# Retention's values in one token-major tile, a flag of their own for the rotation's banks, and a root table loaded earlier

## The reference, cut to what matters

```python
h = rmsnorm(x, mix_norm[l])
u = h @ w_in[l]                        # 1024 -> 3488 columns
(c_x, c_b, c_c, rw_r, rw_k, rw_v, rw_wd_f, rw_wd_b, rw_ad_f, rw_ad_b, rw_gd,
 rt_q, rt_k, rt_v, rt_g, ml_qa, ml_kva) = jnp.split(u, split_points, axis=-1)
...
y_ret = retention_mixer(rt_q, rt_k, rt_v, rt_g, positions, ret_gn_g[l])
y_mla = mla_mixer(ml_qa, ml_kva, positions, mla_q_a_norm[l], mla_q_b[l], mla_kv_a_norm[l], mla_kv_b[l])
```

## The kernel before

| ahead of p | TensorE | VectorE | ScalarE |
|---|---|---|---|
| 6 | MLA's projections (800, 802, 805) | copies of them (978 to 980) | a copy (932) |
| 7 | rotations of MLA (813) and of retention (821) into banks 3 to 7 | MLA's rope (986 to 995) | |
| 8 | | retention's rope (1001, 1002, 1004) | silu of the gates (935) |
| 9 | MLA's scores (829) into banks 3 to 6 | row maxima (1008, 1010) | exponentials (941) |
| 10 | retention's scores (840) | decay (1016), softmax division (1027) | |
| 11 | retention's output (850) | convolution | a square (946) |
| 12 | sums (858), transposes of probabilities (868) | retention's end (1056 to 762) | square root (949), copies (953) |

## Time and profile before

### The profile page before, as it was taken

How to read it: one execution, slowest core, us unless ns; L and a number is a source line. 1 busy time by engine, 2 the same in 40 slices (tenths; PEclk the granted TensorE clock), 3 DMA queues, 4 the chain that set the end, 5 groups by cost and what they waited for, 6 DMA issues and landing times.

```text
span 2914.4 us, 49969 instructions
## 1 busy us (share of the span) xinstructions
PE 2703.1 (93%) x20144; PEld 2382.9 (82%) x20144; DVE 1911.3 (66%) x1750; ACT 1419.3 (49%) x1330; POOL 84.6 (3%) x82
## 2 busy tenths in 40 slices
PE   8999989999999989986999896899999989999997
PEld 8988888989998879976999795687777777777876
DVE  4555765555555854555556645688878878888886
ACT  4343513343343513342336532566757666666665
POOL 6000005000000000000000000000000000000000
PEclk9999999999999999997999998899999999999999
DMA  7553213545553205542555400799989989999995
GB/s 274 181 191 130 93 46 130 187 159 174 187 189 107 94 17 184 187 156 87 187 187 146 145 3 8 283 338 344 344 292 340 342 296 336 337 342 336 341 346 197
DMA packets 340994, 602.08 MB, mean 207 GB/s; under 512 B 11968, under 2 KB 178752, under 8 KB 340672
## 3 DMA queue, kind: packets, MB, share of 16 engines
q1 hardware_dynamic: 333184, 590.84, 59.2%
q10 hardware_dynamic: 7616, 8.58, 0.9%
HBM read 598.34 MB, written 1.05 MB: 206 GB/s over the span
## 4 chain that ended last, share of the span: by engine, by line
DMA 54%; PE 22%; DVE 12%; ACT 8%; DVEq 2%; issue 1%; SPq 1%; another core or an unknown queue 0%; ACTq 0%; PEldq 0%; PEld 0%; POOLq 0%
DMA raw<-in_moe_w_up 26%; DMA raw<-in_ffn_w_down 22%; DVE wlo L285 8%; ACT whi L282 6%; PE ps L781 5%; PE ps L665 3%; DMA raw<-in_w_in 2%; PE ps L419 2%; PE ps L434 1%; PE ps L381 1%; DMA raw<-in_dn_w_out 1%; DMA raw<-in_dn_w_in 1%; DMA raw<-in_pool_w_in 1%; PE ps L1144 1%; PE ps L1131 1%
## 5 line engine op out<-in xcount | busy, mean ns | idle before, releaser
L285 DVE TENSOR_TENSOR wlo<-raw,whi 128x2048 fp32r<-128x2048 f32 x562 | 1286.4, 2289 | 623.1 <-ACT whi L282 621.7
L282 ACT CAST whi<-raw 128x2048 fp32r<-128x2048 f32 x562 | 1071.5, 1907 | 686.0 <-DMA raw<-in_ffn_w_down 171.5
L419 PE MATMUL ps<-xhi,whi 128*128 128x256 f32 x1760 | 500.4, 284 | 2.5 <-DVE xlo L369 2.5
L419 PE MATMUL ps<-xlo,whi 128*128 128x256 f32 x1760 | 498.7, 283 | 0.0
L419 PE MATMUL ps<-xhi,wlo 128*128 128x256 f32 x1760 | 498.7, 283 | 0.0
L2474 PE MATMUL ps<-whi,xhi 128*128 128x512 f32 x896 | 367.6, 410 | 21.3 <-remote 20.1
L2474 PE MATMUL ps<-whi,xlo 128*128 128x512 f32 x896 | 352.6, 394 | 0.0
L2474 PE MATMUL ps<-wlo,xhi 128*128 128x512 f32 x896 | 352.3, 393 | 0.0
L419 PEld LDWEIGHTS ps<-xhi,whi 128*128 128x128 f32 x1760 | 338.0, 192 | 5.2 <-DVE xlo L369 2.7
L419 PEld LDWEIGHTS ps<-xhi,wlo 128*128 128x128 f32 x1760 | 338.0, 192 | 1.9
L419 PEld LDWEIGHTS ps<-xlo,whi 128*128 128x128 f32 x1760 | 338.0, 192 | 0.0
(11 more groups left out here) (498 smaller groups left out, 3780.3 us busy)
## 6 DMA issues: line engine op xcount, KB each, us to landing
raw<-in_moe_w_gate SPq DMA_DIRECT2D x112, 1024.0 KB, 5.1
raw<-in_moe_w_up SPq DMA_DIRECT2D x112, 1024.0 KB, 5.1
raw<-in_moe_w_down SPq DMA_DIRECT2D x112, 1024.0 KB, 4.9
raw<-in_ffn_w_gate SPq DMA_DIRECT2D x55, 1024.0 KB, 5.0
raw<-in_ffn_w_up SPq DMA_DIRECT2D x55, 1024.0 KB, 5.0
raw<-in_ffn_w_down SPq DMA_DIRECT2D x55, 1024.0 KB, 4.8
raw<-in_w_in SPq DMA_DIRECT2D x26, 1024.0 KB, 5.0
raw<-in_dn_w_in SPq DMA_DIRECT2D x16, 1024.0 KB, 5.6
```

The costliest lines, as they stand in the source:

```text
L282: act.copy(whi[:, n % SPLIT, 0:width], raw[:, n % RAW, 0:width]).then_inc(hi_ready[n % SPLIT], 1)
L285: dve.tensor_tensor(wlo[:, n % SPLIT, 0:width], raw[:, n % RAW, 0:width], whi[:, n % SPLIT, 0:width], ALU.subtract).then_inc(split_ready[n ...
L419: mm = pe.matmul(dst[:, b * ntok:(b + 1) * ntok], w[:, n % SPLIT, c * GW + b * P:c * GW + (b + 1) * P], xt[part][:, c, 0:ntok], start=(c = ...
```

## The change

Four edits, all in the mixing stage.

1. **Blocks of tiles.** A table `IN_BLOCKS` says which two blocks a tile holds. Tile 9 now holds blocks 19 and 20, all of the values; tile 10 holds blocks 18 and 21, which don't lie side by side and are loaded by `load_two` with two DMAs of 128 columns each. The order has tile 10 ahead of tile 9. The values' tile is made with x stationary and 256 moving columns, 48 matmuls; tile 10 by the ordinary line, 48 matmuls.
2. **A flag for the banks.** Retention's rope is cut in two. Its first operation, the one that reads banks 6 and 7, goes to the place behind MLA's rope (ahead of p = 7) and raises `rot_read`. MLA's scores wait for `rot_read` in place of `roped`; retention's scores, one position later, wait for `roped`.
3. **Root table.** ScalarE computes one square root of a constant ahead of p = 10, so that the table of square roots is loaded there and not ahead of p = 12.
4. The silu of the gates waits for 6 second halves and no longer for 7, and `ret_out_tensor` takes its values from the new layout.

The diff, cut to its core:

```diff
+        def load_two(sp, n, srcs):
+            take(sp, raw_free[n % RAW])
+            dst = raw[:, n % RAW, :].rearrange("p (c b f) -> p c b f", c=C, b=2)
+            for b, src in enumerate(srcs):
+                sp.dma_start(dst[:, :, b, :], src).then_inc(raw_landed[n % RAW], 16)
...
-        IN_ORDER = (11, 12, 13, 7, 8, 9, 10, 0, 1, 2, 4, 6, 3, 5)
+        IN_BLOCKS = [(2 * j, 2 * j + 1) for j in range(IN_TILES)]
+        IN_BLOCKS[9], IN_BLOCKS[10] = (U_RV, U_RV + 1), (U_RK + 1, U_RG)
+        IN_ORDER = (11, 12, 13, 7, 8, 10, 9, 0, 1, 2, 4, 6, 3, 5)
...
-                        if b in in_token_major(j):
-                            for t in range(TT):
-                                mm = pe.matmul(ps[:, bank_, b * S + t * P:b * S + (t + 1) * P], xt[:, c, t * P:(t + 1) * P], wv,
-                                               start=first and t == 0, stop=last, skip_group_check=True)
...
+            if IN_BLOCKS[j][0] == U_RV:
+                for t in range(TT):
+                    for c in range(C):
+                        for k, (wp, part) in enumerate(PASSES):
+                            mm = pe.matmul(half_of(bank_, t), (xhi, xlo)[part][:, c, t * P:(t + 1) * P],
+                                           wp[:, n % SPLIT, c * GW:(c + 1) * GW], start=(c == 0 and k == 0),
+                                           stop=(c == C - 1 and k == 2))
...
         def mla_scores_tensor(pe):
             pe.wait_ge(f["mla_roped"], 1)
-            pe.wait_ge(f["roped"], 1)
+            pe.wait_ge(f["rot_read"], 1)
...
         def ret_scores_tensor(pe):
+            pe.wait_ge(f["roped"], 1)
...
-                    act.wait_ge(f["in_dve"], 7)
+                    act.wait_ge(f["in_dve"], 6)
...
+                elif p == 10:
+                    act.activation(tiny[:, 72:73], small("one"), ACT.Sqrt)
...
+        def ret_turned_vector(dve):
+            dve.wait_ge(f["rot"], 1)
+            dve.tensor_tensor(ret_tmp, halves_of(6, 2), bc(rope[:, SIN64, :], 4), ALU.mult).then_inc(f["rot_read"], 1)
+
         def ret_rope_vector(dve):
             q = U[:, U_RQ:U_RQ + 4, :]
-            dve.wait_ge(f["rot"], 1)
-            dve.tensor_tensor(ret_tmp, halves_of(6, 2), bc(rope[:, SIN64, :], 4), ALU.mult)
             dve.tensor_tensor(q, q, bc(rope[:, COS64, :], 4), ALU.mult)
             dve.drain()
             dve.tensor_tensor(q, q, ret_tmp, ALU.add).then_inc(f["roped"], 1)
...
                 elif p == 7:
                     mla_rope_vector(dve)
+                    ret_turned_vector(dve)
```

More of the change, by code:

```diff
@@ L767, in mix_tile @@
             width, bank_ = tile_width(j, IN_W), n % SPLIT
[L768 to L775, removed]
-                        if b in in_token_major(j):
-                            for t in range(TT):
-                                mm = pe.matmul(ps[:, bank_, b * S + t * P:b * S + (t + 1) * P], xt[:, c, t * P:(t + 1) * P], wv,
-                                               start=first and t == 0, stop=last, skip_group_check=True)
-                        else:
-                            mm = pe.matmul(half_of(bank_, b, slice(0, m)), wv, xt[:, c, :], start=first, stop=last)
+            if IN_BLOCKS[j][0] == U_RV:
[5 more added lines that the diff above has]
+                                           stop=(c == C - 1 and k == 2))
+            else:
+                for b, (at, m) in enumerate(in_starts(j)):
+                    for c in range(C):
+                        if fresh and b == 0:
+                            wait_xt(pe, c)
+                        for k, (wp, part) in enumerate(PASSES):
+                            mm = pe.matmul(half_of(bank_, b, slice(0, m)), wp[:, n % SPLIT, c * width + at:c * width + at + m],
+                                           (xhi, xlo)[part][:, c, :], start=(c == 0 and k == 0), stop=(c == C - 1 and k == 2))
             mm.then_inc(tile_done[n % SPLIT], 1)
@@ L785, in mix_in_stream @@
             for p, j in enumerate(IN_ORDER):
-                load_tile(sp, n + p, cols(w["w_in"], l * D, j * GW, tile_width(j, IN_W)))
+                at, other = IN_BLOCKS[j]
+                if other == at + 1:
+                    load_tile(sp, n + p, cols(w["w_in"], l * D, at * P, tile_width(j, IN_W)))
+                else:
+                    load_two(sp, n + p, [cols(w["w_in"], l * D, block * P, P) for block in (at, other)])
             return n + IN_TILES
@@ L960, in mix_in_scalar @@
                 take(act, tile_done[m % SPLIT])
-                act.copy(U[:, 2 * j, :], half_of(m % SPLIT, 0)).then_inc(f["in_act"], 1)
-                split_hi(act, m + SPLIT, in_width(p + SPLIT))
+                act.copy(U[:, IN_BLOCKS[j][0], :], half_of(m % SPLIT, 0)).then_inc(f["in_act"], 1)
+                split_hi(act, m + SPLIT, in_width(p + SPLIT), in_landed(p + SPLIT))
             return n + IN_TILES
@@ L1094, in mix_in_vector @@
                 take(dve, hi_ready[m % SPLIT])
-                dve.tensor_copy(U[rows, 2 * j + 1, :], half_of(m % SPLIT, 1, rows)).then_inc(f["in_dve"], 1)
+                dve.tensor_copy(U[rows, IN_BLOCKS[j][1], :], half_of(m % SPLIT, 1, rows)).then_inc(f["in_dve"], 1)
                 split_lo(dve, m + SPLIT, in_width(p + SPLIT))
```

12 lines of the change are left out of this document (6 added, 6 removed).

## The result

| | before | after |
|---|---|---|
| median of 4 runs, us | 2916.41 (2914.81 to 2918.55) | 2886.69 (2884.9 to 2887.23) |
| the profiled execution, its own time | 2916.18 | 2887.08 |
| its span | 2914.4 | 2885.3 |
| mean granted TensorE clock | 0.969 | 0.972 |

The ratio is 0.9897, 95% interval 0.9881 to 0.9912, so the change saves 29.7 us. 2889 was forecast, and the range of 2884 to 2899 holds the result.

A forecast was written before the change was run, and what follows sets the result against it. TensorE, busy 93% of the span, was taken to bound the kernel, with two waits and low clock behind them. 4.8 + 3.3 + 2.9 + 1.3 + 1.5 - 0.4 = 13.4 us a layer, 26.8 in two, gave 2889 us, range 2884 to 2899.

The forecast's parts named there:

- edit 1, two tiles: Tiles of blocks 18 to 21: 48 wide matmuls each, 5.81 us instead of 8.23, saving 4.8 us a layer.
- the scores' wait: TensorE ahead of MLA's scores: `rot_read` is up 3.0 us early, so the whole 3.3 us wait goes.
- the clock behind it: MLA's scores: without idle ahead the clock stays full, 3.46 us instead of 6.40, saving 2.9 us.
- root table: ScalarE ahead of position 12: the table load hides in idle before position 10, saving 1.3 us a layer.
- the clock behind the transposes: Last transposes and the tile behind: an idle of about 1.0 us keeps the clock, saving 1.5 us, bounds 0 and 1.6.
- new stalls: Retention's scores and output wait for later exponentials and decay: 0.4 us lost a layer, bounds 0 and 1.2.
- row of 5.81 us: Profiled whole tile with 256 moving columns and stationary weights, taken as the price of both new tiles.
- The rival that columns set the price: Values' and neighbouring tile: moving columns price a matmul, so the new blocks save nothing; 2899 us, chance 0.04.
- The second rival: MLA's scores still wait, now for `rot_read`, and the clock falls; up to 2901 us, chance 0.07.
- The range from the bounds: Whole kernel: 2886 to 2893 us, given as the forecast's own range from its terms' bounds, chance 0.65.
- I let the gain pass to the end undiminished: Behind the mixing stage: the recurrence follows by the same waits, so all 13.4 us a layer reach the end.

The follow-up runs named there:

- e4: Kernel before with only position 5's tile loaded in two DMAs of 128 columns each, in the old blocks: 2914.54 us, ratio 1.0.
- e7: Kernel before with ten matmuls of zeros on TensorE ahead of the wait of MLA's scores: 2904.81 us, ratio 0.996.
- e3: Kernel before with only the table of square roots loaded ahead of position 10: 2909.07 us, ratio 0.9984.
- e9: Changed kernel with the banks' flag undone, so MLA's scores wait for `roped` again: 2894.72 us, ratio 0.9923.
- e10: Changed kernel with VectorE's row maxima of MLA's scores ahead of position 8's copy and split: 2883.87 us, ratio 0.9888.
- e1: Kernel before with only the new blocks of tiles, their loads and wait counts: 2902.0 us, ratio 0.9959.
- e2: Kernel before with only the read of the rotation's banks moved forward under its own flag: 2902.23 us, ratio 0.9962.
- e8: Changed kernel without the early root table, which loads ahead of position 12 as before: 2891.35 us, ratio 0.9918.
- e5: Kernel before, unchanged, profiled once more: 2916.42 us, ratio 1.0001.
- e6: Changed kernel, unchanged, profiled once more: 2885.02 us, ratio 0.9891.
- e11: Changed kernel with retention's square root ahead of ScalarE's split of the same position: 2882.92 us, ratio 0.9888.
- e12: Changed kernel with both the maxima moved ahead of position 8's split and the root ahead of ScalarE's split: 2882.63 us, ratio 0.9883.

## Why the prediction was right

**By its own steps**, first layer. The stage starts 1.07 us later in the span of after (at 210.31 us against 209.24), so the times of the forecast are read with that added.

| term | forecast | measured | from |
|---|---|---|---|
| edit 1, two tiles | 4.8 | 5.0 | 2 x (8.23 - 5.75) |
| the scores' wait | 3.3 | 3.3 | no wait left |
| the clock behind it | 2.9 | 2.9 | 6.40 - 3.46 |
| root table | 1.3 | 1.3 | wait 2.3 to 0.9 us |
| the clock behind the transposes | 1.5 | 1.5 | 7.87 - (0.63 + 5.74) |
| new stalls | -0.4 | -1.05 | 0.54 + 0.51 |
| sum | 13.4 | 13.0 | stage by its ends: 13.1 |

**Edit 1.** The values' tile costs 5.75 / 48 = 0.120 us a matmul, and the other tile the same 5.75 us, slightly under the row of 5.81 us that I used. The rival that columns set the price would have left both at their old time; it fell. By the gap formula in "TensorE: Matmul & The Clock Gate", section "Back-to-back issue gap", of the Trainium skill the edit would have saved nothing. That section gives the formula for an isolated matmul and says that it under-counts at small N where each matmul has its weight load, so the Trainium skill didn't speak against the edit as the prediction has it. By its section "LDWEIGHTS" 48 loads fewer are worth 5.1 us; 5.0 were measured. The second load of the tile is hidden, as costed: e4 gives a ratio of 1.0.

**The wait for the banks.** VectorE around the flag in the changed kernel, in order of time (start, us, what). L1017 reads the banks, L1023 ends retention's rope, L292 is the split behind position 8's copy, L1027 the maxima, L1035 the decay:

```profile
276.85 1.23 DVE L1017 TENSOR_TENSOR work<-ps,rope 128x1024 f32<-128x1024 f32 x1
...
282.04 1.23 DVE L1023 TENSOR_TENSOR U<-U,work 128x1024 f32<-128x1024 f32 x1
...
283.80 2.28 DVE L292 TENSOR_TENSOR wlo<-raw,whi 128x2048 fp32r<-128x2048 f32 x1
286.22 2.29 DVE L1027 TENSOR_REDUCE tiny<-ps 128x8 f32<-128x2048 f32 x1
...
297.59 2.48 DVE L1035 SCALAR_TENSOR_TENSOR work<-ps,work 128x512 f32<-128x512 f32 x4 [0.21 <-issue]
```

L1017 ends at 278.1 us and the scores start at 281.0: 3.0 us of slack, the forecast figure. The second rival, that the change wouldn't do what it says, needed over 3.0 us more on this chain. Retention's rope ends at 283.3 us and its new waiter, retention's scores, starts at 290.25, so that wait is free, as forecast.

**The clock behind the scores.** The step was right, and e7 shows it nearly by itself, with 1.2 us of the idle left: the same wait, filled with matmuls, gives the scores back 2.7 us. I had treated 6.40 us as the price behind this wait, while the twelve layers of this study that have the wait unfilled lie between 5.38 and 6.85. In the profile that I worked from the price happened to be near the middle.

**The root table.** ScalarE in the changed kernel, in order of time (idle before in the brackets). L960 is the added root with its load, L978 the copy of position 10, L966 the root that counts:

```profile
294.63 1.28 ACT L960 ACT_TABLE_LOAD   x1
...
298.88 0.37 ACT L978 COPY U<-ps 128x256 f32<-128x256 f32 x1 [2.75 <-PE ps L790]
...
309.36 0.68 ACT L966 ACTIVATE work<-ps,con 128x512 f32<-128x512 f32 x1
```

The load lies ahead of the wait for position 10's tile, as costed, and 2.75 us of that idle are left (3.5 forecast). L966 starts on the heels of its split (307.53 to 309.46 us) with no load between.

**The clock behind the transposes.** Right in this pair of profiles, and right in its choice: behind an idle of 0.9 us the clock held in all ten layers that have one (both profiles of after, e3, e9, e10). But the 1.5 us that the edit is paid for depend on the clock having fallen before, and this is not certain. Of the fourteen layers with an idle of 2.3 us at this place it fell in eight (the tile took 6.71 to 7.25 us) and held in six (5.74 or 5.75 us). On the fourteen the term is worth some 0.9 us on average (8/14 x 1.5). In the kernel before it fell four times in four.

The fourteen are not alike. In the eight layers in which TensorE had idled 3.3 us ahead of the scores (both profiles of before, e4, e1) the clock fell here in seven. In the six in which it hadn't (e2, e8) or in which the wait was filled (e7) the clock fell in one. By these layers most of the 1.5 us that the sum gave to edit 3 comes already with edit 2. That leaves the sum of the whole change as it is and moves worth from one edit to the other. Why the earlier idle matters here isn't shown, and fourteen layers are few.

The term's two parts were off and cancelled: 0.43 us for the transposes at full clock where 0.63 were measured, and 5.9 us for the tile where it took 5.74.

**What is new and late** is the one step that was mis-sized. The dates in it were right: exponentials 288.79 to 292.55 us (forecast 289.1 to 292.8 with the 1.07 added), decay ended at 300.07 us (300.2), TensorE at retention's output at 298.76 (298.5). What was wrong is the price behind a late release. I took a quarter of the step for its last head, 0.48 us. The step ended at 301.20 us, 1.13 us behind the decay. Retention's scores read the same: the last head is released by the sixth exponential at 291.64 us and ends at 292.82, 1.18 us later. So a release that comes late costs about 0.65 us more than the last head's share of a step that flows, and both stalls together were 1.05 us, near the upper bound of 1.2. e10 takes the cause away by an earlier start of the maxima, and both are gone.

**The range from the bounds** doesn't follow from them. With every term at its better bound a layer gains 5.3 + 3.3 + 2.9 + 1.3 + 1.6 = 14.4 us, which gives 2887.2; with every term at its worse bound it gains 3.4, which gives 2909. The prediction has 2886 to 2893 as "its own range from the bounds". The measured 2886.7 lies even beyond the better end, by what was gained outside the stage.

**"I let the gain pass to the end undiminished"** is the step that the traces bear out least. All loads and steps behind the stage follow as said, and VectorE has 2.6 us to spare at the last tile (2 forecast). But between two executions the recurrence's own low clock moves by some 2 us, and the last part differs by 6.2 us in favour of the changed kernel. Both were unknown to the sum, and so the 2 us between forecast and median are closer than the working deserves.

**Do the edits add up?** In medians they do: 12.9 + 12.7 + 5.8 = 31.4 us from e1 to e3, against 29.7 and 31.6 for the whole change in its two sets of runs. That is partly chance, as the sections show. In the mixing sections they don't: 11.5 + 12.5 + 6.3 = 30.3 against 25.0. The difference can be read off: the clock behind the transposes was gained by e2 in both layers and by e1 in one although neither has edit 3 (3 x 1.5), and the scores' clock in e1 differs by 1.0 and -0.4 us from before. That leaves 25.2.

**What stays open: the last part.** Its lengths are, for before, e5, e4 and e3, 1120.3, 1117.6, 1117.6 and 1117.0 us; for e7, e1 and e8 1116.5, 1116.5 and 1116.4; for after, e6, e9, e10, e11 and e12 1114.1, 1111.0, 1114.2, 1114.2, 1114.1 and 1114.2; for e2 1113.3. One piece of it is visible. At the turns of the expert loop ScalarE's split waits for a weight tile whose load SyncE issues late. ScalarE and SyncE in the kernel before, in order of time:

```profile
2123.65 1.91 ACT L282 CAST whi<-raw 128x2048 fp32r<-128x2048 f32 x1 [10.52 <-DMA raw<-in_moe_w_up]
```

```profile
2115.20 13.37 SPq L268 DMA_DIRECT2D raw<-in_moe_w_up  x2
```

and in the changed kernel:

```profile
2098.16 1.91 ACT L289 CAST whi<-raw 128x2048 fp32r<-128x2048 f32 x1 [8.30 <-DMA raw<-in_moe_w_up]
```

SyncE's same row has 11.15 us there instead of 13.37.

In each profile there are two such waits (and an earlier one of 6.4 us, which is 4.9 in e6, where the last part is shortest). They are either short, 7.5 to 9.0 us, or long, 10.2 to 10.5: both long in before, one long in e5 (10.4, 8.0), which is the same kernel, and one each in e3 and e4; both short in after (8.3, 7.7), e6, e1, e2 and e7 to e12. My theory was that SyncE's longer program in the changed kernel sets this. It fell: e4 has SyncE's two loads and one long wait, and e2 has SyncE's old program and none. That it differs between two executions of one kernel says that it isn't a property of the change alone; that the changed kernel and its variants never showed a long one says that it may not be chance alone. The waits themselves explain 4.8 of the 6.2 us (10.5 + 10.3 - 8.3 - 7.7). More of the lower clock comes with them: in 16 us around each wait the mean granted clock was 0.68 in before and 0.79 in after. Counted from the start of the last part, the split behind the first wait starts at 329.6 us in before and 327.0 in after, and the one behind the second at 599.2 and 593.6. So 5.6 of the 6.2 us arise at these two places. Why the waits are short in the changed kernel isn't settled.

## What to carry to other kernels

Count matmuls and weight loads before columns: where the stationary operand changes with each matmul, a matmul of 256 columns cost 0.120 us and one of 128 cost 0.111, so the same product with half as many instructions takes little over half the time. Give the reader of a PSUM bank a flag of its own when the next writer waits only for the bank, and price a wait on TensorE together with the low clock behind it, here 3.3 + 2.9 us, but as a price that varies from one execution to the next. When a stall goes, date the next release on every engine in the chain, and price a release that comes late by what a step takes from such a release to its end (here 1.13 and 1.18 us), not by its share of a step that flows. Where two idles follow each other, don't give each its own clock term before both are measured together.

## What the runs showed of the hardware

- **The same idle doesn't always cost the same.** An idle of 2.3 us ahead of the same four transposes was followed by the lower clock in eight layers of fourteen, in e1 and e8 in one layer and not in the other of a single execution. It fell in seven of the eight layers that had an idle of 3.3 us ahead of the scores, and in one of the six that didn't. 0.9 us were followed by none in ten layers. After the 3.3 us idle the clock fell in all twelve layers that have it, for a part of the scores that varied: 5.38 to 6.85 us. Two stretches of e1 at its scores (granted clock is the third number from the end) show how short a fall can be:

```profile
285.00:287.00 2.00, 2.00 (x7) 1.61 (x6) 0.56 (x1) 0.00 (x0) 0.00 (x0) 0.55 0.16 12
287.00:289.00 2.00, 2.00 (x14) 1.82 (x13) 0.41 (x1) 0.00 (x0) 0.00 (x0) 1.00 0.88 285
```

  The first is at 0.55, so almost all at 1.2 GHz; the next is wholly at 2.4 GHz again.
- **A late release costs more than its work.** The last head of a step took 1.13 and 1.18 us from its release to the step's end, against 0.48 and 0.51 us as a quarter of the step in flow.
- **The weight stream pauses at the turns of the expert loop**, for 7.5 to 9.0 or for 10.2 to 10.5 us (ScalarE's wait), and which of the two varies between executions of one kernel. Around each wait of 8.8 us or more the mean granted clock over 16 us was 0.68, around each of up to 8.3 us it was 0.79.
